# One masked decay row per query block, later adds of halves, and a four-to-three split of the PSUM banks in an attention loop

## The reference, cut to what matters

```python
def fox_prompt(q, k, v, logf):
    c = jnp.cumsum(logf.astype(F32), axis=1)     # c: decay per key
    ...
    return fox_attend(qb, cb, t0 + jnp.arange(Q_BLOCK), k, v, c, kpos)
def nsa_prompt(q, nkv, lw):
    ...
    o_c, o_s = nsa_cmp_slc(qb, qpos, kc, vc, ks, vs, table)
    o_w = nsa_window(qb, qpos, kwb, vwb, t0 - WINDOW + jnp.arange(WINDOW + Q_BLOCK), table)
```

## Time and profile before

| quantity | value |
|---|---|
| three runs, us | 1268.25, 1268.99 (median), 1269.88 |
| the profiled execution, us | 1263.59, of which 1261.7 is the span from the first instruction to the last |
| TensorE busy over the span | 1133.6 us, 90% |
| VectorE, ScalarE, GpSimd busy over the span | 735.6, 419.0, 172.2 us |
| mean granted TensorE clock | 0.958 of full |
| attention loop in the trace | about 540 to 756 us |
| TensorE, VectorE, ScalarE busy in 540 to 756 | 176.38, 173.85, 157.10 us of 216 |

### The profile page before, as it was taken

The page is one execution under the profiler, slowest core; times in us unless marked ns, Lnnn a source line. Parts: engine busy times, 40 slices in busy tenths (PEclk is TensorE's granted clock), DMA queues, the critical chain, the costliest instruction groups (busy, mean ns, idle before and its releaser), DMA issues.

```text
span 1261.7 us, 22191 instructions
## 1 busy us (share of the span) xinstructions
PE 1133.6 (90%) x8047; PEld 675.4 (54%) x8047; DVE 735.6 (58%) x1732; ACT 419.0 (33%) x985; POOL 172.2 (14%) x189
## 2 busy tenths in 40 slices
PE   6999999999999999888788889999829999999970
PEld 4676776867866455666565664545423333333320
DVE  6935665855745012578889773436775443344786
ACT  4322524424323010347777771312301110111431
POOL 0122031210311000210000000000000111112243
PEclk9999999999999999979999999999859999999995
DMA  9851030130201303221620007400467978577994
GB/s 288 263 141 31 21 83 3 37 64 20 85 1 52 122 5 63 97 56 29 171 62 2 18 19 211 140 39 17 144 237 258 339 260 291 210 257 255 345 329 160
DMA packets 127320, 164.84 MB, mean 131 GB/s; under 512 B 32257, under 2 KB 101201, under 8 KB 127222
## 3 DMA queue, kind: packets, MB, share of 16 engines
q1 hardware_dynamic: 112070, 109.91, 28.9%
q0 software_dynamic: 15152, 53.60, 11.7%
HBM read 226.35 MB, written 36.47 MB: 208 GB/s over the span
## 4 chain that ended last, share of the span: by engine, by line
PE 75%; DVE 13%; DMA 4%; issue 3%; ACT 2%; SPq 1%; POOL 0%; DVEq 0%; POOLq 0%; ACTq 0%
PE act L743 18%; PE vec L1366 10%; PE vec L778 8%; PE vec L1092 8%; PE vec L753 5%; PE vec L999 4%; PE act L1014 3%; PE vec L794 2%; DVE arena L2107 2%; PE vec L1379 2%; PE act L1379 2%; DMA arena<-x_rows,arena 2%; PE act L1026 2%; DVE arena L2123 1%; PE act L1039 1%
## 5 line engine op out<-in xcount | busy, mean ns | idle before, releaser
L743 PE MATMUL act<-arena 128*128 128x352 f32 x768 | 236.9, 463 | 1.2 <-ACT arena L1460 1.2
L743 PEld LDWEIGHTS act<-arena 128*128 128x128 f32 x768 | 143.1, 190 | 77.6 <-ACT arena L1460 1.7
L1366 PE MATMUL vec<-arena 128*64 128x512 f32 x768 | 172.8, 601 | 1.6 <-DMA arena<-in_exp_w 1.6
L1092 PE MATMUL vec<-arena 128*128 128x512 f32 x256 | 112.9, 594 | 0.8 <-DVE arena L2132 0.8
L1366 PEld LDWEIGHTS vec<-arena 128*64 128x64 f32 x768 | 53.4, 138 | 101.6 <-issue 99.9
L778 PE MATMUL vec<-arena 128*128 128x512 f32 (+1 forms) x256 | 100.3, 546 | 0.0
L1604 ACT COPY arena<-act 128x64 f32<-128x64 f32 (+7 forms) x256 | 70.9, 361 | 50.6 <-PE act L1014 50.5
L1614 ACT ACTIVATE arena<-arena 128x640 f32<-128x640 f32 (+15 forms) x128 | 82.3, 657 | 10.0 <-DVE arena L2107 9.1
L2457 DVE TENSOR_SCALAR arena<-arena 128x256 f32<-128x256 f32 x24 | 7.1, 296 | 129.3 <-ACT arena L1711 129.3
L1092 PEld LDWEIGHTS vec<-arena 128*128 128x128 f32 x256 | 47.4, 189 | 58.2 <-issue 56.8
L2107 DVE CUSTOM_DVE_ANT_0 arena<-vec,arena 128x128 f32<-128x128 f32 (+6 forms) x168 | 68.9, 430 | 16.1 <-PE vec L999 5.8
(11 more groups left out here) (461 smaller groups left out, 1875.3 us busy)
## 6 DMA issues: line engine op xcount, KB each, us to landing
arena<-in_exp_w SPq DMA_DIRECT2D x192, 512.0 KB
arena<-in_exp_w SPq DMA_DIRECT2D x48, 1024.0 KB
y_rows<-arena POOLq DMA_DIRECT2D x24, 512.0 KB, 6.0
arena<-in_w_in SPq DMA_DIRECT2D x16, 512.0 KB, 6.7
arena<-in_x_prompt SPq DMA_DIRECT2D x8, 512.0 KB, 6.4
x_spill<-arena POOLq DMA_DIRECT2D x8, 512.0 KB, 3.2
arena<-x_spill SPq DMA_DIRECT2D x8, 512.0 KB, 5.1
arena<-in_cache_fox_kv SPq DMA_DIRECT2D x16, 256.0 KB, 3.5
```

What stands on the lines that cost most here:

```text
L743: last = mm(bk[:, 0:n], W[k % 2][:, c, m * P:(m + 1) * P], xT[:, c, a:a + n], start=c == 0, stop=c == NC - 1)
L1092: last = mm(bk[:r], src, Wo[half][:, c, :], start=c == 0, stop=c == NC - 1)
L1366: last = mm(gu_bank[p][o], xgT[p][:, c, o], Wgu[:, slot, c, :], start=c == 0, stop=c == NC - 1)
```

## The change

**Decay rows.** In place of `cumf` and `foxdiag` each head has two whole copies of the decay row, `fox_rows[h % 2][0]` and `[1]`, loaded by two transfers (for head 0 the second is a GpSimd copy of 128 x 1024). Query block i uses copy i % 2, in which only block i carries the mask. GpSimd masks one block of 128 x 128 at a time, two blocks ahead, and after the fox scores of block i puts back the plain values there by a copy of 128 x 128. A fox chunk is always one piece. VectorE's scores of a long item wait for the mask of its block and for the restored block i-2.

**Halves.** VectorE's `add_halves` moves from the end of step d (even, for item d-3) to step d+1, behind `scores(d+1)` and ahead of `normalise(d)`.

**Banks.** The ring `turned` gets four banks (the fourth is `vec[3]`); the scores of the loop and of the small matmuls around it go through a new ring `score` with the three banks `vec[0:3]`. TensorE waits once, ahead of the loop, until the ring `vec` is empty.

```diff
-    banks["turned"], banks["summed"] = banks["act"][0:3], banks["act"][3:4]
+    banks["turned"], banks["summed"] = [*banks["act"][0:3], banks["vec"][3]], banks["act"][3:4]
+    banks["score"] = banks["vec"][0:3]
...
-    cumf, foxdiag = [z.take(1024) for _ in range(2)], [z.take(SEQ, 8) for _ in range(2)]
+    fox_rows = [[z.take(SEQ) for _ in range(2)] for _ in range(2)]
...
         if kind == "fox":
-            off = min(n, i * P - a)
-            whole = [(0, off, cumf[h % 2][:, a:a + off])] if off > 0 else []
-            return whole + ([(n - P, P, foxdiag[h % 2][:, i, :])] if a + n == L else [])
+            return [(0, n, fox_rows[h % 2][i % 2][:, a:a + n])]
...
         def load_decay(h):
-            e.dma_start(cumf[h % 2], bcast(decay_rows[8 * h:8 * h + 8], SEQ)).then_inc(*E.moved(f"cumf{h % 2}_in", ("cumf", h)))
+            for copy in fox_rows[h % 2]:
+                e.dma_start(copy, bcast(decay_rows[8 * h:8 * h + 8], SEQ)).then_inc(*E.moved(f"cumf{h % 2}_in", ("cumf", h)))
...
         E.stage("p3")
+        e.wait_ge(*E.emptied("vec"))
...
-                e.wait_ge(*E.free("vec"))
-                bk = E.bank("vec")
+                e.wait_ge(*E.free("score"))
+                bk = E.bank("score")
...
             if d % 2 == 0:
-                e.wait_ge(*E.at(("foxdiag", h)))
+                e.wait_ge(*E.at(("diagonal masked", h, i)))
+                if i >= 2:
+                    e.wait_ge(*E.at(("row restored", h, i - 2)))
...
+            if it >= 5 and it % 2:
+                add_halves(it - 4)
             if 2 <= it <= n:
                 normalise(it - 1)
-            if it >= 4 and it % 2 == 0:
-                add_halves(it - 3)
+        add_halves(n - 1)
...
+        def mask_diagonal(h, i):
+            row = fox_rows[h % 2][i % 2][:, i * P:(i + 1) * P]
+            tt(row, row, C["diagmask"], ALU.add).then_inc(*E.done(("diagonal masked", h, i)))
...
+            if d == 0:
+                e.wait_ge(*E.at(("cumf", 0)))
+                e.tensor_copy(fox_rows[0][1], fox_rows[0][0]).then_inc(*E.done())
+                e.wait_ge(*E.own())
+                mask_diagonal(0, 0)
+                mask_diagonal(0, 1)
+            if kinds[0] == "fox" and i + 2 < 8:
+                mask_diagonal(h, i + 2)
+                e.wait_ge(*E.at(("scores", d, 0)))
+                used, plain = (fox_rows[h % 2][x][:, i * P:(i + 1) * P] for x in (i % 2, 1 - i % 2))
+                e.tensor_copy(used, plain).then_inc(*E.done(("row restored", h, i)))
             if d % 16 == 9 and h + 1 < H:
                 e.wait_ge(*E.at(("cumf", h + 1)))
-                tt(foxdiag[(h + 1) % 2], cumf[(h + 1) % 2].rearrange("p (t k) -> p t k", t=8), C["diagmask"].unsqueeze(1).to_broadcast([P, 8, P]), ALU.add).then_inc(*E.done(("foxdiag", h + 1)))
+                mask_diagonal(h + 1, 0)
+                mask_diagonal(h + 1, 1)
```

More of the change, by code:

```diff
@@ L981, in first_decay_rows @@
                     last = mm(bk[:, c * P:(c + 1) * P], lf, C["negtri"], start=True, stop=True)
-                last.then_inc(*E.filled("vec"))
+                last.then_inc(*E.filled("score"))
         def scores(d):
@@ L995, in scores @@
                     k = {"fox": KT[0:64, h], "slc": KT[64:128, 0], "cmp": KC[64:128]}[kind][:, a:]
[L996 to L997 removed]
+                e.wait_ge(*E.free("score"))
+                bk = E.bank("score")
                 events = [("queries read", h)] if d % 16 == 15 else []
[L999 removed]
+                mm(bk[:, 0:n], q[s, h, i * P:(i + 1) * P], k[:, 0:n], start=True, stop=True).then_inc(*E.filled("score", *events))
         def transposes(d):
@@ L2020, in gelu_inner @@
             x, u = gx[:, o:o + HALF_GELU], gu[:, o:o + HALF_GELU]
-            e.wait_ge(*E.full("vec"))
-            bk = E.job("vec")
+            e.wait_ge(*E.full("score"))
+            bk = E.job("score")
             cp(pc[:, kv:kv + 1], bk[:, 64:65]).then_inc(*E.done())
```

73 lines of the change are left out of this document (33 added, 40 removed).

## The result

The changed kernel takes **1293.2 us** (median of four runs, 1292.5 to 1293.8) against 1268.6 (1267.1 to 1269.9): a ratio of 1.0194 with an interval of 1.0177 to 1.0212, or +24.6 us.

A forecast was written before the change was run, and what follows sets the result against it. Two loops of equal length, one through VectorE alone, one through add of halves, values and next scores, were taken as the bound. 27.7 - 6.4 + 0 - 1.2 + 1.7 = +21.8 us on 1269.0 gave 1290.8, range 1277 to 1306.

The forecast's parts named there:

- The start of VectorE and TensorE together: At 741.05, block 6 of the last head: both engines ready together, VectorE starting 1.30 us after TensorE's first score matmul.
- the rival that TensorE's loop has slack: Attention loop: VectorE alone sets its start, so the later add brings no waits; 1261 us, chance 8%.
- the covered case: VectorE needs only the first score chunk, so each wait is 0.43 us shorter; 1280 us, chance 12%.
- The later add, +27.7: Long items' values wait for the add, delaying next long scores; waits 7.1 us a head, +27.7 us over four heads.
- One piece, -6.4: Fox chunks in blocks 1, 2, 3, 5, 6, 7: 24 fewer VectorE instructions at 0.27 us each, -6.4 us.
- GpSimd, +1.7: Small masks and copies, about 0.4 us each, partly uncovered, against VectorE hold-ups removed: +1.7 us net, ends -7 and +20.
- The upper end of the term (+20) and its rival: GpSimd masks and copies slow, at 0.9 us an operation: +20 us as term end, 1305 us as rival, chance 5%.
- The banks, 0: Three score banks, blocks 4 to 7: TensorE waits 0.7 us for the first bank, costed at 0, upper end +5 us.
- four banks remove ScalarE's stops, which are not on the loop, so 0: Four transpose banks remove stops for ScalarE's copies between two groups, in TensorE's even step, off the bounding loop: 0.
- The boundaries, -1.2: Three head boundaries: next scores go before the add, so block 1 starts 0.4 us sooner; -1.2 us, between 0 and -6.6.
- its rival came in part: TensorE's added idling lowers its clock, some 2 us a hit block, one to three more a head; 1299 to 1315, chance 14%.

The follow-up runs named there:

- the one with the early add: The changed kernel with the add of halves back in its place of before, decay rows and banks kept: 1262.5 us, ratio 0.9973 against the kernel before.
- The two kernels with two banks of sums: The changed kernel with two banks for sums and three for turned blocks, add of halves late or in its old place: 1276.8 and 1276.1 us.
- three, three and one: The changed kernel with the add of halves in its old place, three banks for turned blocks, three for scores, one for sums, one idle: 1275.1 us.

## Why the prediction was right

1291 was predicted, 1293.2 measured. The terms, in its order:

- **The start of VectorE and TensorE together** in the earlier trace rows. Right: the 1.30 us came back at the same place with 1.19 of it marked as a wait. The reading that an unmarked start was set by both engines was what the rest hung on, and the rival that TensorE's loop has slack fell with the later add alone, +31.5. So did the covered case, which had each wait 0.43 us shorter.
- **The later add, +27.7.** Right in place and mechanism, and near in size. In the last head the waits ahead of the long scores of blocks 2 to 7 are 0.55, 1.27, 0.95, 1.03, 1.12 and 1.19. The forecast counts them as the waits of blocks 1 to 6 (the block normalised just before): 0.73, 0.94, 1.09, 1.17, 1.21 and 1.22. Together 6.1 against 6.4. Between the changed kernel and the one with the early add lie 28.0 us, forecast 27.7 - 1.2 = 26.5; but some of the 28 is clock (below), so that the waits alone came out a little under the forecast. The two kernels with two banks of sums show why: the values wait for the bank.
- **One piece, -6.4.** Right in kind, its size not shown. 168 score instructions became 144 (143 in the rows, whose window leaves out one that begins at 539.6), and their group fell by 5.1 us, to which 24 reads of the least value go, at 0.08 us each. But busy time is not time on the loop. From long scores to long scores the kernel with the decay rows alone is, in most heads, 0.25 to 0.28 us shorter in blocks 1, 5 and 6, as forecast, but only 0.16 to 0.18 in block 3, about 0.1 in block 7 and 0.02 to 0.04 in block 2; block 4, where three masks meet, is 0.2 to 0.4 longer. These lengths hold what the masks cost as well.
- **GpSimd, +1.7. Too high by what the medians say.** The decay rows alone gave -7.5 (-10.9 to -4.1) where -6.4 and +1.7 make -4.7; the interval just holds that. With one piece at its full 6.4 the middle puts this term at -1; the runs do not separate the two. One block, the second head's block 4, holds 3.2 us of the gain: before, it has the pair of 2.80 us of the earlier trace rows and a granted clock of 0.67 in 624 to 628. The upper end of the term (+20) and its rival do not agree: with +20 in the sum the rival is at 1309, not 1305. The operations are about as short as assumed, 0.48 us a mask in the mean (0.45 in the median) and 0.29 a copy:

```profile
L2617 POOL TENSOR_TENSOR arena<-arena 128x128 f32<-128x128 f32 x32 | 14.9, 477 | 0.1
L2633 POOL COPY arena<-arena 128x128 f32<-128x128 f32 x24 | 7.0, 292 | 116.8 <-DVE arena L2110 116.8
```

  What they take from VectorE is small: the first instruction of a normalisation that stands beside a mask takes 0.39, 0.26 or 0.36 us instead of 0.16. The long operations of the earlier trace rows held up VectorE for up to 2.2 us (2.80 instead of 0.64); the short ones for 0.1 to 0.25. The Trainium skill (GPSIMD Engine Reference, section Specifications) says that GpSimd's SBUF interfaces are shared with VectorE, with contention where a VectorE instruction runs in a two-port mode or has two inputs in SBUF. The short operations fit that, since the first instruction of a normalisation has two inputs in SBUF; in which mode the long pair of the earlier trace rows ran, which has one, no row shows. That every normalisation is hit did not come: the median of these 64 instructions is 0.16 us.
- **The banks, 0. Under-sized.** Alone they cost 4.4 us (1.1 to 7.7). The working looked at blocks 4 to 7, where its 0 came out on balance only (block 7 +0.57 us three times, the boundary behind it 0.5 less); it left out the head of the loop, where the same ring carries the hidden values and decay rows, and where three banks cost VectorE 3.1 us in the kernel with the banks alone and 4.4 in the changed one. The term "four banks remove ScalarE's stops, which are not on the loop, so 0" was right for four score banks and wrong for three: three, three and one shows that the fourth turned bank is worth some 11 us there, a part of it clock. The two errors do not show in the sum, because the change has both sides of the split.
- **The boundaries, -1.2.** Not tested by itself. Waits ahead of adds fell by 6.5, but waits ahead of block 0's and 1's scores took their place. With its own wait of 0.76 a boundary was forecast to be 0.36 us longer. From the long scores of block 7 to those of block 1 the late add made the three boundaries 0.0, 0.4 and 0.0 us longer with three score banks (the changed kernel against the one with the early add), and 0.5 to 0.7 us with four (on the decay rows alone).
- **The clock.** The prediction gave it no term, and its rival came in part. From 572 us to the loop's end the granted clock means 0.98 before, 1.00 in the changed kernel with the early add and 0.96 in the changed kernel. There TensorE stood at the low level for a part of five places. Two of them, columns as in the earlier trace rows:

```profile
636.00:640.00 4.00, 3.97 (x22) 2.27 (x18) 1.30 (x4) 0.87 (x4) 0.00 (x0) 0.59 0.00 0
692.00:696.00 4.00, 2.86 (x28) 2.21 (x30) 2.64 (x11) 2.87 (x12) 0.00 (x0) 0.74 0.00 0
```

  They lie in block 4 of the second and third head, which takes 9.49 and 9.30 us where the last head's takes 7.52: 1.8 to 2.0 us each, the "some 2 us" of the rival, but in two blocks in all and not in one to three a head; the other three places cost less than 1 us each. By the same comparison of blocks, the five places cost some 6 us (an estimate) of the 30 by which the blocks of this trace are longer than with the early add. In most blocks TensorE stood for 0.9 us or more and the clock stayed at 1.00.
- **The rest of the profile.** The two profiled executions differ by 29.5 us where 21.8 were forecast, and the loop is 245 us long instead of 237. In the account above the 8 us are the head of the loop (+5.6, forecast 0) and ScalarE's exponentials (+4.1, forecast 0), less some 2 at scores and adds, which already hold the low clock's share; why the exponentials came late more often wasn't taken apart.

By the runs the account is: later add +28.0, banks +4.1 (0.9973 less 0.9941), decay rows -7.5, sum 24.6. The sum comes out by construction, since each term is the step from one kernel to the next, and another order gives other terms: added last, the banks are at -1.3 (1.0194 less 1.0204), and the later add on the rows alone is at +33.4. The forecast had +26.5, 0 and -4.7. The errors of its parts, 1.5, 4.1 and 2.8 us, are of both signs and partly cancel. So the mechanism was right, and that the total is within 3 us is in part luck.

## What to carry to other kernels

Where two engines are ready at the same moment, no wait is marked, and yet either may not be delayed: compare the start with a marked one elsewhere before you call an engine free. An operation that frees the only PSUM bank of its ring belongs as early as it can go; how late it may come is the room behind it, and a second bank makes its place of no account. Count a ring's banks for every stage that uses the ring, the head of a loop too, and count stops in pairs: one of 0.6 us a block was free beside four score banks, and beside three it cost 0.5 to 0.7 in the three longest blocks of a head. And an edit of the order of steps may move another instruction than the one meant, as at the head boundaries: read in the trace which one moved.

## What the runs showed of the hardware

- VectorE started on the first of several queued score matmuls of 512 columns 1.30 to 1.31 us after TensorE began it, in three kernels, also with a 16-column matmul in second place. The cause is open.
- GpSimd: a copy of 128 x 1024 took 1.03 us (at 537.89 after the change) and an add of that shape 2.35; at 128 x 128 a copy took 0.29 and an add 0.45 in the median.
- A value matmul started 0.14 to 0.16 us after the end of the VectorE add that freed its bank, in all 31 places of the changed kernel.
- The same 32 matmuls took 5.48 us behind one wait of 1.35 us, at a granted clock of 1.00, and 8.30 us behind two waits of 1.27 and 1.23, at 0.65, which is a mix of the two levels of 2.4 and 1.2 GHz.
